# Turning the softmax weights with VectorE and HBM in place of TensorE, in a four-layer encoder

## The reference

```python
# differential attention, per head h and block of 128 queries
logits = jnp.einsum('bqhmd,bkhmd->bmhqk', qb, k).astype(jnp.float32) + bias
probs = jax.nn.softmax(logits, axis=-1)
w = (probs[:, 0] - lam * probs[:, 1]).astype(v.dtype)
return jnp.einsum('bhqk,bkhe->bqhe', w, v)

# cross-attention, in every layer
logits = jnp.einsum('bshd,bmhd->bhsm', q, km).astype(jnp.float32)
probs = jax.nn.softmax(logits, axis=-1).astype(vm.dtype)
return jnp.einsum('bhsm,bmhd->bshd', probs, vm).reshape(b, s, XATTN_W)
```

## Time and profile before

| | |
|---|---|
| median of 3 runs | 1246.14 us (1246.03 to 1246.64) |
| the profiled execution, span | 1244.7 us |
| TensorE matmuls busy | 1235.2 us, 99% |
| VectorE busy | 1024.4 us, 82% |
| ScalarE busy | 730.3 us, 59% |
| POOL busy | 20.1 us, 2% |
| DMA engines busy, mean | 55.9% (229.27 MB, 184 GB/s) |

### The profile page before, as it was taken

The page is one execution under the profiler, slowest core; times in us unless marked ns, Lnnn a source line. Parts: engine busy times, 40 slices in busy tenths (PEclk is TensorE's granted clock), DMA queues, the critical chain, the costliest instruction groups (busy, mean ns, idle before and its releaser), DMA issues.

```text
span 1244.7 us, 19689 instructions
## 1 busy us (share of the span) xinstructions
PE 1235.2 (99%) x7370; PEld 1082.9 (87%) x7370; DVE 1024.4 (82%) x1599; ACT 730.3 (59%) x1190; POOL 20.1 (2%) x29
## 2 busy tenths in 40 slices
PE   9999999999999999999999999999999999999997
PEld 7988888888999988888889888888888888888886
DVE  5876888889779888988887978988888776988887
ACT  6675765555766546555555546655554774755552
POOL 0001000000000100000000000000000001000000
PEclk9999999999999999999999999999999999999999
DMA  9834576554553345655655764656554533666651
GB/s 333 285 120 136 190 248 190 186 192 163 175 182 119 122 150 169 227 187 195 201 173 168 233 204 162 227 195 199 190 186 169 187 119 119 218 207 201 196 190 54
DMA packets 64539, 229.27 MB, mean 184 GB/s; under 512 B 7575, under 2 KB 9239, under 8 KB 63421
## 3 DMA queue, kind: packets, MB, share of 16 engines
q1 hardware_dynamic: 64444, 228.02, 55.5%
HBM read 226.93 MB, written 1.06 MB: 183 GB/s over the span
## 4 chain that ended last, share of the span: by engine, by line
PE 97%; DMA 1%; SPq 1%; DVE 0%; issue 0%; ACT 0%; DVEq 0%
PE pair L768 28%; PE acc L862 21%; PE pair L771 14%; PE pair L800 4%; PE pair L801 4%; PE pair L802 4%; PE acc L768 2%; PE acc L843 2%; PE acc L842 2%; PE acc L841 2%; PE pair L1022 2%; DMA raw<-in_stream 1%; PE pair L825 1%; PE pair L827 1%; PE pair L829 1%; PE acc L931 1%
## 5 line engine op out<-in xcount | busy, mean ns | idle before, releaser
L1278 DVE TENSOR_TENSOR w_lo<-raw,w_hi 128x1024 fp32r<-128x1024 f32 x400 | 482.6, 1221 | 105.3 <-ACT w_hi L1040 103.7
L1040 ACT ACTIVATE w_hi<-raw 128x1024 fp32r<-128x1024 f32 x400 | 420.5, 1058 | 213.2 <-PE pair L771 70.8
L768 PE MATMUL pair<-xT,w_hi 128*128 128x512 f32 x1520 | 477.8, 396 | 0.0
L771 PEld LDWEIGHTS pair<-xT,w_lo 128*128 128x128 f32 x1520 | 285.5, 188 | 67.2
L771 PE MATMUL pair<-xT,w_lo 128*128 128x256 f32 x1520 | 298.6, 278 | 0.0
L768 PEld LDWEIGHTS pair<-xT,w_hi 128*128 128x128 f32 x1520 | 233.8, 189 | 3.2 <-issue 0.3
L1087 ACT ACTIVATE hid<-pair 128x512 f32<-128x512 f32 x88 | 52.6, 597 | 124.9 <-PE pair L771 124.9
L1319 DVE TENSOR_TENSOR hid<-pair,hid 128x512 f32<-128x512 f32 x88 | 60.7, 690 | 47.9 <-ACT hid L1087 47.7
L800 PE MATMUL pair<-xT,w_hi 128*128 128x256 f32 x336 | 97.8, 291 | 0.0
L801 PE MATMUL pair<-xT,w_hi 128*128 128x256 f32 x336 | 95.0, 283 | 0.0
L802 PE MATMUL pair<-xT,w_lo 128*128 128x256 f32 x336 | 94.9, 283 | 0.0
(11 more groups left out here) (223 smaller groups left out, 1661.9 us busy)
## 6 DMA issues: line engine op xcount, KB each, us to landing
raw<-in_stream SPq DMA_DIRECT2D x400, 512.0 KB, 4.6
gains<-in_ln SPq DMA_DIRECT2D x8, 1024.0 KB, 8.4
bias<-bias_scratch SPq DMA_DIRECT2D x2, 1152.0 KB, 9.0
raw<-in_stream SPq DMA_DIRECT2D x8, 256.0 KB, 6.6
x_tok<-in_x_t SPq DMA_DIRECT2D x4, 256.0 KB, 6.2
y_tok<-in_mem_t SPq DMA_DIRECT2D x2, 512.0 KB, 7.1
x_tok<-in_x SPq DMA_DIRECT2D x1, 1024.0 KB, 6.5
out<-x_tok SPq DMA_DIRECT2D x4, 256.0 KB, 2.0
```

Of the source, the lines that this page charges most:

```text
L768: pe.matmul(bank, w_hi[:, slot, kk * P:(kk + 1) * P], xT[:, kk].rearrange("p a s -> p (a s)"), start=(kk == 0), stop=(kk == KT - 1), skip_ ...
L771: last = pe.matmul(bank[:, 0:SEQ], w_lo[:, slot, kk * P:(kk + 1) * P], xT[:, kk, 0, :], start=False, stop=(kk == KT - 1), skip_group_check ...
L1040: nc.scalar.activation(w_hi[:, u % SPLIT, :], raw[:, u % RAW, :], ACT.Copy).then_inc(hi_ready, 1)
L1278: v.tensor_tensor(w_lo[:, u % SPLIT, :], raw[:, u % RAW, :], w_hi[:, u % SPLIT, :].bitcast(F32), ALU.subtract).then_inc(lo_ready, 1)
```

## The change

TensorE's transposes and their copies out of PSUM go away. VectorE transposes the weights in blocks of 32x32 (items `xswap` and `swap`, an instruction each) into a buffer: `ex` for cross-attention, the free half of the `prob` slot for heads. POOL stores this to a scratch tensor in HBM with four DMAs, one for each group of 32 partitions, and `xfetch` or `fetch`, also on POOL, loads it back with the block rows and columns exchanged. The cross-attention product reads what landed directly, with its columns in another order; for heads ScalarE copies it into `probT` (item `spread`). In the hgrn layer ScalarE, not VectorE, multiplies by the inverse sums. SP's loop over the units is rewritten as a walk over the items, with the same loads in the same order. Some items move: the last two `pv`, `ms`, `tok` and `scale` of the attention layers.

```diff
-                  6: [it("exp", 0), it("xturn", 0)], 7: [it("exp", 1), it("xpv", 0)],
...
-                  16: [it("scale", 0), it("prob", 5)], 18: [it("turnw", 4), it("pv", 2), it("pv", 3), it("turnw", 5)],
-                  19: [it("pv", 4), it("pv", 5), it("ms", 1), it("tok", 1), it("ms", 2)], 20: [it("scale", 1), it("tok", 2)],
-                  21: [it("scale", 2)]}
+            at = {0: [it("xlog", 0), it("xlog", 1)], 1: [it("xexp", 0)], 2: [it("xexp", 1), it("xprob", 0), it("xswap", 0)],
+                  3: [it("xprob", 1), it("xswap", 1), it("xfetch", 0)], 4: [it("xfetch", 1)],
+                  5: [it("log", 0), it("log", 1)], 6: [it("exp", 0)], 7: [it("exp", 1), it("xpv", 0)],
...
+                  16: [it("scale", 0), it("prob", 5), it("swap", 5), it("fetch", 4)], 17: [it("fetch", 5)],
+                  18: [it("pv", 2), it("pv", 3)], 19: [it("ms", 1), it("tok", 1)],
+                  20: [it("scale", 1), it("pv", 4), it("pv", 5)], 21: [it("ms", 2), it("tok", 2)],
+                  22: [it("scale", 2)]}
+            for h, n in ((11, 0), (12, 1), (14, 2), (15, 3), (18, 4), (19, 5)):
+                at[h].append(it("spread", n))
...
-                  4: [it("xturn", 0)], 5: [it("xpv", 0)], 8: [it("xturn", 1)], 9: [it("xpv", 1)]}
+            at = {0: [it("xlog", 0), it("xexp", 0), it("xlog", 1), it("xexp", 1)],
+                  1: [it("xprob", 0), it("xswap", 0), it("xprob", 1), it("xswap", 1)],
+                  2: [it("xfetch", 0)], 3: [it("xfetch", 1)], 5: [it("xpv", 0)], 9: [it("xpv", 1)]}
...
-                  4: [it("xturn", 0)], 5: [it("xpv", 0)], 6: [it("xturn", 1)], 7: [it("xpv", 1)]}
+                  2: [it("xswap", 0), it("xswap", 1)], 3: [it("xfetch", 0), it("xfetch", 1)],
+                  5: [it("xpv", 0)], 7: [it("xpv", 1)]}
...
+        def swap_source(n):
+
+            s = n % 2
+            return (ex[:, s] if items[prob_pos[n]][0] == "xprob" else prob[:, s, 1:2]).rearrange("p i t s -> p (i t s)")
...
-                    pe.wait_ge(xprobT_ready, 2 * u + 2)
+                    n = weights_of(item)
+                    pe.wait_ge(swap_landed[n % 2], 16 * (n // 2 + 1))
...
-                                             xprobT[:, i, k, :], start=(k == 0), stop=(k == 1))
+                                             weights[:, i, k], start=(k == 0), stop=(k == 1))
...
+                elif name == "xprob" and layer_kind(item[1]) == "hgrn":
+                    n = weights_of(("xswap",) + item[1:])
+                    act.wait_ge(inv_ready, item[2] + 1)
+                    for i in range(2):
+                        for t in range(TT):
+                            j = 2 * i + t
+                            last = nc.scalar.activation(prob[:, n % 2, i, t, :], ex[:, n % 2, i, t, :], ACT.Copy,
+                                                        scale=row_inv[:, n % 2, j:j + 1])
+                    last.then_inc(xprob_ready, 1)
+                elif name == "spread":
+                    n = weights_of(item)
+                    act.wait_ge(swap_landed[n % 2], 16 * (n // 2 + 1))
+                    nc.scalar.activation(probT[:, item[2]].rearrange("p t k (a j) -> p (t k) a j", a=4),
+                                         swap_target(n).rearrange("p a (c j) -> p c a j", j=32), ACT.Copy).then_inc(probT_ready, 1)
...
+                        before, layer, h = items[prob_pos[n - 2]]
+                        if before == "prob":
+                            dve.wait_ge(probT_ready, HEADS * (layer // 3) + h + 1)
...
+                elif name in ("xswap", "swap"):
...
+                    v.transpose(swap_source(n).rearrange("p (b c j) -> p c b j", b=4, j=32),
+                                of.rearrange("p i t (k b j) -> p (i t) k b j", k=2, j=32)).then_inc(swapped, 1)
...
+                elif name in ("xswap", "swap"):
+                    n = weights_of(item)
+                    pool.wait_ge(swapped, n + 1)
+                    for a in range(4):
+                        rows = slice(32 * a, 32 * a + 32)
+                        nc.gpsimd.dma_start(swap_scratch[n][a].rearrange("b i e -> i b e"), swap_source(n)[rows].rearrange(
+                            "i (b e) -> i b e", b=4)).then_inc(swap_stored[n % 2], 16)
+                elif name in ("xfetch", "fetch"):
...
+                    pool.wait_ge(swap_stored[n % 2], 64 * (n // 2 + 1))
+                    nc.gpsimd.dma_start(swap_target(n), swap_scratch[n].rearrange("a b i e -> (b i) a e")).then_inc(swap_landed[n % 2], 16)
```

More of the change, by code:

```diff
@@ L653, in _ @@
                     load_bias()
+            for item in items:
+                name = item[0]
+                if name == "begin" and item[1] % 2:
+                    next_unit(item[1] // 2 * 2 + item[2] + RAW)
+                elif name == "lo":
+                    next_unit(item[1] + RAW)
             for t in range(TT):
@@ L1525, in _ @@
                 elif name in ("xprob", "prob"):
-                    n = prob_ord[pos]
+                    n = weights_of((name.replace("prob", "swap"),) + item[1:])
                     s = n % 2
```

134 lines of the change are left out of this document (61 added, 73 removed).

## The result

The changed kernel takes 1337.38 us (median, 1333.67 to 1339.8), the kernel before 1246.2 us beside it: a ratio of 1.073, 95% interval 1.071 to 1.075. The forecast was 1256.2 with a range of 1240 to 1279. The sign is right; the size is nine times the forecast's: 91 us lost where 10 were expected.

The account below looks back on a forecast made before the run. TensorE, busy 1235.2 of 1244.7 us, was taken to bound the kernel. Stalls of 22.4 us less a gain of 12.3 us gave +10.1 us on the profiled 1244.7, that is 1256.2 beside the median, range 1240 to 1279.

Parts of the forecast that it names:

- The gain of 12.3 us: TensorE loses eight groups of eight transposes at 0.88 us and twelve groups of four at 0.44 us: 7.0 + 5.3.
- Prices t and the transposes: Issue of a DMA on POOL, t, 0.55 us (0.33 to 1.24); VectorE's transposes 1.2 and 0.7 us.
- rival of dear issue: VectorE holds POOL up so that each DMA issue takes 1.24 us: 1278.8 us or more, chance 0.10.
- The stall sum, 22.4 us: TensorE's stalls: conv 7.5, hgrn 5.2, layer 0 2.0, layer 3 1.2, last heads 5.6, last scales 0.9 us.
- L: Landing time of a load from HBM: at least 2.0 us, at most 4.6, the weight loads' median; 4.6 taken.
- dear end: Issue at 1.24 us and load landing at 4.6 us: stalls of 45.0 us and a time of 1278.8 us.
- Last heads, 5.6 + 0.9 us: Both attention layers: the last heads' product stalls 2.8 us twice, the chain behind the last scale 0.45 us twice.
- Hidden by the units four halves ahead: VectorE's added 15.6 us of transposes cost nothing, covered by units of weights prepared four halves ahead.
- The clock: Rival: after the two long stalls TensorE runs at 1.2 GHz as long as it rested: 1262.6 us, chance 0.12.
- short round trips: Rival: cheaper issue and landing on the path through HBM make the change faster, down to 1240.2 us, chance 0.20.
- everything hidden: Rival: VectorE and ScalarE run far enough ahead that no stall remains: 1233.8 us, chance 0.04.
- break-even: Rival: the time stays within 2.5 us of 1246.14, chance 0.12.

Follow-up runs that it names:

- e14: e12 with the conv layer's cross-attention products moved from slots 11 and 13 to 13 and 15: 1246.42 us, ratio 1.0003 to the kernel before.
- e1: The changed kernel with dynamic_dma_scratch_size, the memory for POOL's DMAs, raised from 1024 to 2048 bytes: 1307.1 us.
- e5: e1, and SyncE issues no load of weights between a layer's first swap and the landing of its load: 1291.06 us.
- e8: The kernel before with only heads 0 to 3 of both attention layers through HBM, at 2048 bytes: 1253.3 us, ratio 1.0057.
- e9: e8 with ScalarE's spread of head 2 one slot later: 1248.74 us.
- e4: The kernel before with the 20 VectorE transposes added as dead work, TensorE's own transposes kept: 1250.77 us, ratio 1.0038.
- e10: e1 with the cross-attention products of the conv and hgrn layers placed in later slots: 1290.54 us.
- e3: The changed kernel with filler matmuls on TensorE ahead of its wait for each layer's first cross-attention weights: 1329.7 us.
- e12: The kernel before with only hgrn and conv cross-attention weights through HBM, 2048 bytes, products later, conv's VectorE transposes in slots 3 and 5: 1251.94 us.
- e7: The changed kernel at 1024 bytes with only the heads' weights through HBM, cross-attention weights transposed by TensorE as before: 1283.98 us.
- e11: e9 plus the cross-attention weights of hgrn and conv through HBM, with the later product slots of e10: 1251.02 us, ratio 1.0045.
- e2: e1 with the load reading whole rows, 128 pieces in place of 512, so the weights land in another order: 1303.0 us.

## Why the prediction was right or wrong, point by point

- **The bound and the sign: right.** TensorE had no slack, every stall counted in full, and slower was given 0.64. Of the forecast's places the first product of each layer is one in the trace too, with the longest wait in the conv layer, and no second product waits. The product of the fifth head is none.
- **The gain of 12.3 us: consistent, not measured by itself.** 112 transposes are gone from the order. In e14 32 of them went with 2.6 us of new waits at an unchanged time, which fits 0.88 us for each group of eight (3.5 in all) to about 1 us.
- **Prices t and the transposes: right.** A store's issue takes 0.55 us, with VectorE busy beside it; a load's 0.76. The transposes take 1.25 and 0.71 us against 1.2 and 0.7. That disposes of the rival of dear issue: at no place did a DMA instruction of POOL last 1.24 us. The Trainium skill's trap on VectorE and GpSimd's descriptors (SBUF — State Buffer, "DVE blocks DMA") did not show in these durations.
- **The stall sum, 22.4 us: wrong, and this is the step that failed.** TensorE waited 53.6 us at the first products where the sum had 15.9, and 30.4 in the tails where it had 6.5. It rested on "eight stores issued, load landed *L* later" with *L* = 4.6 at most. In the conv layer the sum was 0.75 + 2.2 + 4.6 = 7.5 us. The trace has 0.7 us from TensorE's coming to the end of the second transpose, 3.2 for the stores, 5.1 until the load starts, and 9.1 until it has landed: 18.2, rounding apart. Two terms were missing. One is the **full memory of POOL's queue**, 30.3 us over the whole kernel (e1). The other is **contention**: the 4.6 us were the weights' landing, taken as an upper end because the bytes were the same. A load that meets the weights' own traffic takes 9.0, with the weights held back it takes 4.5, and the kernel 16.0 us less (e5). The prediction's reason for a short landing, that the stall leaves the weight buffers full, fits only the second load of the changed kernel (4.2 us), and only because that load was held back: in the first 10 us of the stall SyncE still fills them, and in e1 the second load takes 8.5.
- **The range: too narrow for the same reason.** Its dear end kept *L* at 4.6. The median of one kind of load was no upper end: the trace of before also has a load of 512 KB that took 9.0 us, the masks, issued at 19.8 us beside the first weights. The Trainium skill's estimate of 3.2 us pointed the wrong way: 4.5 was measured with the traffic held back, and 9.0 with it.
- **Last heads, 5.6 + 0.9 us: the layers right, the place and the cause not.** The two tails have 30.4 us. Some 12.8 of them stand at the first `scale` and 12.9 at the second, where the sum had nothing, since the middle heads were costed at nothing. The third has 3.3, where the sum had 0.9, and 1.4 stand at the product of the first heads in layer 3. The product of the fifth head, with 5.6 us in the sum, does not wait: it stands right behind the second `scale`, and the weights of heads 4 and 5 are ready by then. The forecast followed the last load only. ScalarE waits 28.9 us in nine places at its spreads (L1246), and w_hi, seeds and exponentials stand behind them in order. The second `scale` of layer 0 shows it, behind the spread of head 4:

```profile
125.66 0.63 ACT L1246 ACTIVATE probT<-prob 128x512 f32<-128x512 f32 x1 [4.46 <-DMA prob<-swap_scratch]
126.19 1.04 ACT L1053 ACTIVATE w_hi<-raw 128x1024 fp32r<-128x1024 f32 x1
127.26 1.23 DVE L1295 TENSOR_TENSOR w_lo<-raw,w_hi 128x1024 fp32r<-128x1024 f32 x1 [8.44 <-ACT w_hi L1053]
...
129.73 0.69 DVE L1593 TENSOR_TENSOR a_out<-a_out,ms_r 128x512 f32<-128x512 f32 x1 [1.16 <-POOL ms_r L1656]
130.48 1.12 PE L1016 MATMUL pair<-ident,a_out 128*128 128x128 f32 x4 [5.50 <-DVE a_out L1593]
```

The prediction said that VectorE's prob would wait for spreads and be covered; it never asked what is queued behind a spread on ScalarE. e8 and e9 show this cause for head 2, 4.6 us; for heads 4 and 5 the trace has the same order, and no run takes it apart.

- **"Hidden by the units four halves ahead": wrong for VectorE.** 15.6 us of transposes cost 4.8 in e4. The cover is for weights; `hid`, `qk` and the cross-attention copies have none: e4's new waits are at these three, and e10 has one for `qd`.
- **The clock: right as a mechanism, wrong as a separate case.** It was a rival with 6 us and 0.12. It is not an alternative to the stalls but comes behind them: 7.7 us for the four first products (e3), and 2.3 us on top of waits of 3.2 (e12 against e14). It does not come behind every one: of e8's two waits at the first `scale`, 3.5 us in layer 0 and 3.3 in layer 3, the first was followed by half clock for some 3 us and the second by full clock. And the low clock did not last as long as the rest before it, as the rival had it: some 6 us behind the 18.2.
- The rivals of short round trips, of everything hidden, and of break-even fell with the first landing. That a column order read with strides costs nothing holds: eight matmuls take 1.08 us at full clock as before.

What stays open: how e1's 30.3 us divide between the memory and the stalls that it hid; whether the hardware queues land faster beside the weights; and how much of the loss in the attention layers (37.7 us in e7) belongs to heads 4 and 5.

## What to carry to other kernels

A round trip through HBM has to be priced with the traffic that runs beside it and with the number of pieces outstanding on its queue, and a wait without a releaser ahead of a DMA instruction was the sign here that this queue was full. When an instruction gets a new wait, list what stands behind it on its own in-order engine, whoever that is: in layer 0 of e8 a copy on ScalarE waited 2.2 us, and TensorE, further on, 3.5. A kernel whose bound engine never rests can pay for a stall twice, once for the wait and once for the clock behind it (3.2 us of waits cost 5.5 in e12), so a saving of 12 us on TensorE can't be bought with even a few waits of 3 us.

## What the runs showed of the hardware

- With 1024 bytes POOL's queue took 896 pieces outstanding and not 1024: the eighth store of 128 pieces came 0.5 to 1.5 us late in all four layers, and the second load of 512 waited until the first had landed. With 2048 bytes no such wait was left. Only these counts were seen.
- A DMA instruction of POOL took 0.55 us with 128 pieces and 0.76 with 512. In e2 loads with 128 pieces took 0.56 and 0.55.
- A load of 512 KB in pieces of 1 KB landed in 9.0 us beside the weights and in 4.5 with them held back; in pieces of 4 KB, beside the weights, in 7.7. These are medians of the four first loads; the second ones took 8.5 us with pieces of either size, and 4.3 with the weights held back.
- The time at low clock did not grow with the stall. TensorE's work began at 713.45 behind a wait of 2.9 us in e12, and the clock was 0.50 until 717 and 0.58 until 720; it began at 756.49 behind 18.2 us in the changed kernel, and the clock was 0.57 from 757 to 763.
- A wait of 3.5 us did not always lower the clock: behind the one for `hid` in e11 it was 1.00, behind the one for a_out in layer 0 of e8 it was 0.50 from 92 to 95.
